# Expert rows and expert results as high and low fp32r parts

## The reference

```python
def moe_swiglu(h, w_router, w1, w3, w2):
    logits = (h @ w_router).astype(jnp.float32)
    top_v, top_i = lax.top_k(logits, TOP_K)
    gates = jax.nn.softmax(top_v, axis=-1)
    combine = jnp.sum(jax.nn.one_hot(top_i, N_EXPERTS, dtype=jnp.float32) * gates[..., None], axis=-2)
    out = jnp.zeros_like(h)
    for e in range(N_EXPERTS):
        out = out + combine[..., e:e + 1].astype(h.dtype) * swiglu(h, w1[e], w3[e], w2[e])
    return out
```

## Time and profile before

| | |
|---|---|
| time, median of 3 runs | 1761.59 us (1758.38 to 1762.69) |
| profiled execution | 1761.89 us |
| its span | 1760.0 us |
| TensorE matmuls | 1648.2 us busy, 94% |
| VectorE | 1336.6 us, 76% |
| ScalarE | 1059.4 us, 60% |
| GpSimd | 112.1 us, 6% |
| DMA | 427.99 MB, mean 243 GB/s |

### The profile page before, as it was taken

One profiled execution on the slowest core, in us unless ns is written; L12 is line 12 of the kernel. 1 busy time (PEld: TensorE's weight loads), 2 busy tenths in 40 slices (PEclk: granted clock), 3 DMA queues, 4 the chain that ended last, 5 costly groups with the idle time before them and its releaser, 6 DMA issues.

```text
span 1760.0 us, 27088 instructions
## 1 busy us (share of the span) xinstructions
PE 1648.2 (94%) x9618; PEld 1418.2 (81%) x9618; DVE 1336.6 (76%) x1250; ACT 1059.4 (60%) x1039; POOL 112.1 (6%) x151
## 2 busy tenths in 40 slices
PE   6888969999797897799999999999999999999997
PEld 5877859999797786688888888888888888888886
DVE  4888555444458865788888888888888888888885
ACT  4634454433353335477677677677777777676775
POOL 1142100000005210000000000000000000000000
PEclk8999989999899999799999999999999999999999
DMA  7520036452352103499999999999999999999993
GB/s 230 159 72 25 16 120 216 165 192 95 119 168 71 42 1 118 143 356 363 311 366 351 321 368 358 323 366 356 325 366 338 340 367 327 352 366 328 347 367 114
DMA packets 327137, 427.99 MB, mean 243 GB/s; under 512 B 6849, under 2 KB 294753, under 8 KB 326961
## 3 DMA queue, kind: packets, MB, share of 16 engines
q1 hardware_dynamic: 326304, 425.28, 71.8%
q0 software_dynamic: 640, 2.00, 0.4%
q10 hardware_dynamic: 144, 0.05, 0.0%
HBM read 426.25 MB, written 1.05 MB: 243 GB/s over the span
## 4 chain that ended last, share of the span: by engine, by line
PE 74%; DVE 11%; ACT 5%; issue 5%; DMA 4%; SPq 0%; DVEq 0%; ACTq 0%; POOL 0%; POOLq 0%
PE bank L375 29%; PE bank L400 15%; PE bank L1121 8%; PE bank L378 7%; PE bank L628 6%; PE bank L403 4%; DMA ring<-in_moe_w 3%; ACT wh L435 2%; DVE wl L439 2%; PE bank L660 1%; PE bank L388 1%; PE bank L1126 1%; DVE ml L615 1%; DVE hs L1877 1%; DVE rw L1779 1%
## 5 line engine op out<-in xcount | busy, mean ns | idle before, releaser
L439 DVE TENSOR_TENSOR wl<-ring,wh 128x2048 fp32r<-128x2048 f32 x369 | 844.6, 2293 | 211.4 <-ACT wh L435 198.8
L435 ACT ACTIVATE wh<-ring 128x2048 fp32r<-128x2048 f32 x369 | 705.9, 1915 | 130.2 <-PE bank L400 43.5
L375 PE MATMUL bank<-wh,xh 128*128 128x512 f32 x896 | 361.7, 404 | 0.9 <-DVE xl L868 0.9
L375 PE MATMUL bank<-wh,xl 128*128 128x512 f32 x896 | 351.1, 392 | 0.0
L375 PE MATMUL bank<-wl,xh 128*128 128x512 f32 x896 | 349.6, 390 | 0.0
L375 PEld LDWEIGHTS bank<-wh,xh 128*128 128x128 f32 x896 | 168.4, 188 | 37.5 <-issue 4.9
L375 PEld LDWEIGHTS bank<-wh,xl 128*128 128x128 f32 x896 | 168.3, 188 | 37.3
L375 PEld LDWEIGHTS bank<-wl,xh 128*128 128x128 f32 x896 | 169.0, 189 | 32.0
L400 PE MATMUL bank<-wh,gh 128*128 128x512 f32 x448 | 175.5, 392 | 3.5 <-DVE gl L525 3.4
L400 PE MATMUL bank<-wh,gl 128*128 128x512 f32 x448 | 174.6, 390 | 0.0
L400 PE MATMUL bank<-wl,gh 128*128 128x512 f32 x448 | 174.6, 390 | 0.0
(11 more groups left out here) (294 smaller groups left out, 2564.3 us busy)
## 6 DMA issues: line engine op xcount, KB each, us to landing
ring<-in_moe_w SPq DMA_DIRECT2D x336, 1024.0 KB, 8.3
ring<-in_ffn_w SPq DMA_DIRECT2D x33, 1024.0 KB, 6.1
ring<-in_w_in SPq DMA_DIRECT2D x24, 1024.0 KB, 5.3
ring<-in_w_out SPq DMA_DIRECT2D x8, 1024.0 KB, 5.1
ring<-in_w_in SPq DMA_DIRECT2D x2, 640.0 KB, 4.0
const<-in_const SPq DMA_DIRECT2D x1, 1200.0 KB, 14.4
proj<-in_x SPq DMA_DIRECT2D x4, 256.0 KB, 6.7
out<-wide SPq DMA_DIRECT2D x1, 1024.0 KB, 4.0
```

The lines of the kernel that those rows point to most:

```text
L375: ins = nc.tensor.matmul(up_bank(run, par, 0)[:], x[:, 0:C], w[b][:, k], **kw)
L435: nc.scalar.activation(o, src[0], ACT.Copy).then_inc(sem("w_high"), 1)
L439: nc.vector.tensor_tensor(split(wl[:, buf]), src[0], split(wh[:, buf]).bitcast(F32), ALU.subtract).then_inc(sem("w_split"), 1)
```

## The change

The rows of h are kept as two tiles, hh and hl, in fp32r, and gather multiplies both with `sel`, now fp32r. The gates leave the scatter matrix: `place`, the plain 0/1 sum, is transposed to `placed`, and the gate of each place comes as a column from two small matmuls of `selg` with ones, is copied to `gslot`, and is applied as a scale when the job's result leaves PSUM, again as two parts, yh (ScalarE) and yl (VectorE, new function `acc_low`). scatter multiplies both with `placed`. `zero_acc` is gone. The first down of a job, and of the dense layer, starts the sums itself, for which step 1 is taken out of the loop. The change's short description also names row-major weights; the diff changes no load of weights.

```diff
+        yh = sb("yh", [P, D], F32R)
+        yl = sb("yl", [P, D], F32R)
+        hh = sb("hh", [P, TT, D], F32R)
+        hl = sb("hl", [P, TT, D], F32R)
+        sel = sb("sel", [P, TT, C], F32R)
...
             n = run.pairs - 1
-            with pe.Fori(0, n // 2) as i:
-                step(2 * i + 1, 1)
+            step(1, 1, True)
+            with pe.Fori(0, (n - 1) // 2) as i:
                 step(2 * i + 2, 0)
-            if n % 2:
-                step(n, 1)
-
-        def zero_acc(banks_):
-            for b in banks_:
-                nc.tensor.matmul(bank[b][:], zeros[:, 0:P], zeros[:, P:P + 512], start=True, stop=True)
+                step(2 * i + 3, 1)
+            if (n - 1) % 2:
+                step(n, 0)
...
-            pe.wait_ge(sem("h_copied"), 4)
+            pe.wait_ge(sem("h_high"), 4)
+            pe.wait_ge(sem("h_low"), 4)
...
-                            mm(bank[5 + half][:, d * C:(d + 1) * C], hrows()[:, tt, k * P:(k + 1) * P], sel[:, tt],
-                               tt == 0, tt == 1, "gathered" if d == 3 and tt else None)
+                            mm(bank[5 + half][:, d * C:(d + 1) * C], hh[:, tt, k * P:(k + 1) * P], sel[:, tt], tt == 0, False)
+                            mm(bank[5 + half][:, d * C:(d + 1) * C], hl[:, tt, k * P:(k + 1) * P], sel[:, tt], False, tt == 1,
+                               "gathered" if d == 3 and tt else None)
...
-                    turn(bank[7][:, tt * P:(tt + 1) * P], selg[:, tt], sig="gates_turned" if tt else None)
+                    turn(bank[7][:, tt * P:(tt + 1) * P], place[:, tt])
+                for tt in range(TT):
+                    mm(bank[7][:, T:T + NE], selg[:, tt], cst("ones")[:, 0:NE], tt == 0, tt == 1, "gates_turned" if tt else None)
...
-                pe.wait_ge(sem("acc_copied"), 2 * j + 2)
+                pe.wait_ge(sem("y_low"), 2 * j + 2)
...
-                        mm(bank[SCATTER[b]][:, k * T:(k + 1) * T], yj[:, dt * P:(dt + 1) * P], pgt[:],
-                           sig="scattered" if k else None)
+                        mm(bank[SCATTER[b]][:, k * T:(k + 1) * T], yh[:, dt * P:(dt + 1) * P], placed[:], True, False)
+                        mm(bank[SCATTER[b]][:, k * T:(k + 1) * T], yl[:, dt * P:(dt + 1) * P], placed[:], False, True,
+                           "scattered" if k else None)
...
                 pe.wait_ge(sem("scatter_added"), 4 * (j - 1) + 2)
-                zero_acc((2, 3))
                 pe_steps(pe, nxt)
...
-                nc.scalar.copy(pgt[:], bank[7][:, 0:T]).then_inc(sem("gates_copied"), 1)
+                nc.scalar.copy(gslot[:], bank[7][:, T:T + 1]).then_inc(sem("gslot_ready"), 1)
+                nc.scalar.activation(placed[:], bank[7][:, 0:T], ACT.Copy).then_inc(sem("gates_copied"), 1)
...
-                    nc.scalar.copy(yj[:, half * 512:(half + 1) * 512], bank[2 + half][:]).then_inc(sem("acc_copied"), 1)
+                    nc.scalar.activation(yh[:, half * 512:(half + 1) * 512], bank[2 + half][:], ACT.Copy, scale=gslot[:, 0:1]
+                                         ).then_inc(sem("y_acc_high"), 1)
...
+            for b in range(4):
+                dve.wait_ge(sem("h_high"), b + 1)
+                hv = slice(b * T, (b + 1) * T)
+                nc.vector.tensor_tensor(hl[:, :, hv], bank[b][:].rearrange("p (a t) -> p a t", a=TT), hh[:, :, hv].bitcast(F32),
+                                        ALU.subtract).then_inc(sem("h_low"), 1)
...
+            def acc_low(j):
+                dve.wait_ge(sem("gslot_ready"), j + 1)
+                for half in range(2):
+                    dve.wait_ge(sem("y_acc_high"), 2 * j + half + 1)
+                    hv = slice(half * 512, (half + 1) * 512)
+                    nc.vector.scalar_tensor_tensor(yl[:, hv], bank[2 + half][:], gslot[:, 0:1], yh[:, hv].bitcast(F32),
+                                                   ALU.mult, ALU.subtract).then_inc(sem("y_low"), 1)
...
                 gathered(j)
                 up(0, 0, 0, 1)
+                acc_low(j - 1)
                 up(1, 0, 1, 0)
...
+                nc.gpsimd.tensor_tensor(place[:], hit[:, 0], hit[:, 1], ALU.add).then_inc(sem("gates_chain"), 1)
```

More of the change, by code:

```diff
@@ L178, in program @@
         hT = sb("hT", [P, KT, T])
-        zeros = sb("zeros", [1, 640], BF16)
         tiny = sb("tiny", [P, 1])
@@ L242, in program @@
         gate = sb("gate", [P, 2, T])
-        yj = sb("yj", [P, D])
-        sel = sb("sel", [P, TT, C])
+        yh = sb("yh", [P, D], F32R)
[3 more added lines that the diff above has]
+        sel = sb("sel", [P, TT, C], F32R)
+        place = sb("place", [P, TT, C])
+        gslot = sb("gslot", [P, 1])
         selg = sb("selg", [P, TT, C])
@@ L248, in program @@
         hit = sb("hit", [P, 2, TT, C])
-        pgt = sb("pgt", [P, T])
+        placed = sb("placed", [P, T], F32R)
         rt = sb("rt", [P, T])
@@ L389, in pe_turn_gated, with pe_down @@
                 ins.then_inc(sem("g_turned"), 1)
-        def pe_down(pe, run, m, last=False):
+        def pe_down(pe, run, m, last=False, first=False):
             stage, buf = run.down(m, last)
@@ L400, in pe_down @@
                             ins = nc.tensor.matmul(bank[2 + o][:], g[:, a, 0:C], w[b][:, a, o * 512:(o + 1) * 512],
-                                                   start=False, stop=False, skip_group_check=True)
+                                                   start=first and a == 0 and g is gh and b == 0, stop=False, skip_group_check=True)
                         else:
@@ L404, in pe_down @@
                                                    w[b][:, a, o * P:(o + 1) * P], g[:, a],
-                                                   start=False, stop=False, skip_group_check=True)
+                                                   start=first and o % 2 == a == b == 0 and g is gh, stop=False, skip_group_check=True)
                 if last and not run.moe and o % 2 and o < KT - 1:
@@ L410, in pe_steps, with step @@
         def pe_steps(pe, run):
-            def step(m, par):
+            def step(m, par, first=False):
                 pe_up(pe, run, m, par, 0)
@@ L415, in step @@
                 pe_up(pe, run, m, par, 1)
-                pe_down(pe, run, m - 1)
+                pe_down(pe, run, m - 1, first=first)
             n = run.pairs - 1
-            with pe.Fori(0, n // 2) as i:
-                step(2 * i + 1, 1)
+            step(1, 1, True)
+            with pe.Fori(0, (n - 1) // 2) as i:
                 step(2 * i + 2, 0)
-            if n % 2:
-                step(n, 1)
-        def zero_acc(banks_):
-            for b in banks_:
-                nc.tensor.matmul(bank[b][:], zeros[:, 0:P], zeros[:, P:P + 512], start=True, stop=True)
+                step(2 * i + 3, 1)
+            if (n - 1) % 2:
+                step(n, 0)
         def split_high(act, stage, buf, src, split):
@@ L552, in pe_ffn_dense @@
         def pe_ffn_dense(pe):
-            zero_acc((2, 3, 4, 5))
             for part in range(2):
@@ L687, in last_job @@
             return eng.value_load(jt[0:1, MAXJOBS + 1:MAXJOBS + 2], min_val=0, max_val=MAXJOBS - 2)
-        def hrows():
-            return wide[:].rearrange("p (a b) t -> p a (b t)", a=TT)
         def pe_moe(pe, mm, turn):
@@ L771, in act_moe @@
                 act.wait_ge(sem("h_turned"), b + 1)
-                copy(hrows()[:, :, b * T:(b + 1) * T], bank[b][:].rearrange("p (a t) -> p a t", a=TT), "h_copied")
+                nc.scalar.activation(hh[:, :, b * T:(b + 1) * T], bank[b][:].rearrange("p (a t) -> p a t", a=TT), ACT.Copy
+                                     ).then_inc(sem("h_high"), 1)
             act.wait_ge(sem("gate_logit"), 1)
@@ L784, in gates @@
                 act.wait_ge(sem("gates_turned"), j + 1)
-                nc.scalar.copy(pgt[:], bank[7][:, 0:T]).then_inc(sem("gates_copied"), 1)
+                nc.scalar.copy(gslot[:], bank[7][:, T:T + 1]).then_inc(sem("gslot_ready"), 1)
+                nc.scalar.activation(placed[:], bank[7][:, 0:T], ACT.Copy).then_inc(sem("gates_copied"), 1)
             def acc(j):
                 act.wait_ge(sem("stage_used"), job(j).down(0, True)[0] + 1)
+                act.wait_ge(sem("gslot_ready"), j + 1)
                 for half in range(2):
-                    nc.scalar.copy(yj[:, half * 512:(half + 1) * 512], bank[2 + half][:]).then_inc(sem("acc_copied"), 1)
+                    nc.scalar.activation(yh[:, half * 512:(half + 1) * 512], bank[2 + half][:], ACT.Copy, scale=gslot[:, 0:1]
+                                         ).then_inc(sem("y_acc_high"), 1)
             last = PAIRS_E - 1
@@ L923, in dve_moe @@
             dve_gated_low(dve, run, last)
+            acc_low(j)
             scattered(j)
@@ L937, in job_matrices @@
                                             ).then_inc(sem("gates_chain"), 1)
-                pool.wait_ge(sem("gates_chain"), 2 * j + 2)
+                pool.wait_ge(sem("gates_chain"), 3 * j + 3)
```

(1 more changed line is left out.)

## The result

The changed kernel takes 1770.78 us (median of 4 runs, 1766.73 to 1772.80), the kernel before 1760.15 beside it (4 runs, 1758.38 to 1762.69). The ratio is 1.0055 [1.0042, 1.0069], so +9.7 us; the two medians are 10.6 us apart. Measured again later on another chip, the changed kernel came out at 1.0044 [1.0027, 1.0061], +7.7 us. The prediction was 1789.3 in a range of 1759 to 1794. The sign was right, the size was not.

The account below looks back on a forecast made before the run. TensorE was taken as the bound, DMA some 6 us per job behind. Terms: 25.6 later downs, -2.3 release, +4.7 before job 0, -0.3 at the end: +27.7, so 1789.3 us; range 1759 to 1794, forecast's own 1784 to 1794.

Parts of the forecast that it names:

- I take 0.223: Gather: each 128-column fp32r matmul costs 0.223 us, as in fp32, so gather takes 7.14 us; held little better than even.
- +3.57 us: Gather at each of the 7 changes of job: TensorE time added by twice as many matmuls at 0.223 us.
- +3.7 at gather(0): Gather before job 0: about +3.7 us, from 0.223 us per matmul at full clock.
- rival A: Gather: 128-column fp32r matmuls cost 0.119 us, gather 3.81 us; sum +1.0, 1763 us; chance 0.36.
- That gather runs half on the slow clock: Gather before job 0: its 32 records take 5.93 us, half at the slow clock.
- Scatter gives nothing: Change of job: scatter's saving of 1.5 us becomes TensorE idle, about 2 us, before the wait for VectorE's second addition.
- The subtractions before job 0: VectorE, before gather(0): four subtractions of 128x512 delay the copy of the positions by 1.0 us.
- The scaled copies: ScalarE's two evacuations of results with a scale pointer: +0.09 us each, +0.2 on the chain per change of job.
- The low parts: VectorE, change of job: two scalar_tensor_tensor of 128x512 from PSUM take 1.4 us, falling into a 1.16 us gap plus 0.2.
- rival C: Change of job: short gather, but VectorE's two low parts find no gap, costing 1.5 us each time; 1773 us; chance 0.06.
- The release chain: Change of job, freeing banks 2 and 3: zeroing gone -0.53, ScalarE +0.2, so -0.33 us per change, -2.3 over 7.
- Rival B: Change of job: release of banks 2 and 3 does not hold TensorE, so scatter's saving counts; 1753 us; chance 0.08.

Follow-up runs that it names:

- The filler: Changed kernel plus 16 matmuls of 256 columns behind each scatter, written to bank 7, which nobody reads then: 1766.94 us, ratio 1.0033.
- the two kernels with filler: Changed kernel plus 16 extra matmuls behind scatter, with gather back in fp32 without subtractions (1761.72 us) or streaming 256 columns in 24 of 32 matmuls (1762.62 us).

## Why the prediction was wrong

**The failed step** is the gather: "I take 0.223". Measured: 0.112. The seven times +3.57 us never came (+0.03 each), and of the +3.7 at gather(0) +1.0 came. Together these terms were 28.7, more than the whole sum of +27.7. The argument "the only row of this very shape on four-byte data" put the shape above the format. The 32 fp32 records, each at 0.112, were already at the distance of the bare weight loads, 0.111: a row that shows a limit says nothing of the price per column beyond it. The Trainium skill's "TensorE: Matmul & The Clock Gate", section LDWEIGHTS, gives P/1.2 ns for a load of P columns, 107 ns for 128; the trace is near it, with 0.112 us over 32 pairs of load and matmul. I had cited it as the lower bound and then not let it decide.

That the sign came out right is luck. The time was forecast from a long gather, and what made the kernel slower is for the most part the clock, whose price the sum did not have. Only the 1.0 us of the subtractions was in it. The range holds the measured time only because it was drawn down to rival A; the forecast's own part of it began at 1784.

**Rival A had the right gather and missed the clock.** It gives 1763 and the median is 1770.8. "That gather runs half on the slow clock" took for granted that the clock would rise during the gather again (before, 4.5 of its 5.65 us were at the low level). With 128-column fp32r matmuls it did not: +1.0 us for the gather and +2.4 for job 0, shown by the gather alone in the old kernel (+5.1 with the subtractions) and taken away by 256 columns. That is 3.1 more than the 0.3 of rival A.

**The idle behind scatter was foreseen and priced at nothing.** "TensorE now idles about 2 us instead of 0.3. Scatter gives nothing" is right on both counts (2.08 us; from scatter to the next step −0.18). But the idle had a price of its own: in three of the profiles with it (one of them the changed kernel's second) the clock fell to 1.2 GHz right behind it, five times in all. The filler, which removes nothing but the idle, gives back 2.3, 3.3 and 5.5 us in three pairs of kernels, the last of them well clear of noise, the first not by itself. Not every such gap does it: the changed kernel's two profiles have seven each and show one fall behind them.

The Trainium skill's "TensorE: Matmul & The Clock Gate", section "Why this matters for your kernels", asks for no idle gaps between bursts of matmuls, with waits for DMA as its case, and the gaps that it warns of are longer than these. Here the clock also fell behind gaps of 2.1 us that a semaphore of VectorE makes, so the measurement decides.

**Steps that held.** The subtractions before job 0: +1.0 forecast, +0.98 measured. The scaled copies: yh 1.27 us for two against 1.07, +0.2 as forecast. The low parts: 1.41 for two, forecast 1.4, inside the gap; rival C is out. The release chain: −0.33 forecast, −0.18 seen. A quiet change in all −0.1 to −0.35, where rival A's terms (0.69 − 0.36 hidden − 0.33) make 0. Rival B is out as a forecast, since the second addition ends 3.9 us after scatter begins (1630.47 against 1626.58), but the wait that it names is where the time lies: with the wait moved, 8 us or so came back.

**How the 9.7 us divide.** By experiments: 4.4 to 5.1 for the gather's part (the gather alone), 2.3 to 5.5 for the clock behind the idle. What is left is about 2 us by the ratios, as in the two kernels with filler. The parts do not add up exactly: with the gather back in fp32 the ratio only went from 1.0055 or 1.0044 to 1.0036, less than the gather's part, and the two profiles of the changed kernel differ in where the clock falls. Part of the rest is the run's last stretch. After the last job TensorE waits 2.2 us for the low parts, and no filler stands there. In five of the ten profiles with this wait the clock falls again, 0.7 to 1.5 us after the wait ends. From the last transposes of gated values to the end these five take 25.5 to 25.6 us; the other profiles take 24.3 to 24.7. That was not tested alone. Also open: the profiles show one execution each, and how often the clock falls in the others can't be read, only that the changed kernel's mean clock is 0.968 to 0.971 against 0.972 to 0.976 before; and why in the first profile it fell at 1110.8, after an idle of 0.9 us, before scatter.

## What to carry to other kernels

When fp32 matmuls of few columns become pairs of fp32r matmuls, compare both with the distance of the bare weight loads first. Here both stood at that limit, and the change was worth nothing. Time saved on TensorE ahead of a fixed wait turns into idle, and the idle may be worse than the work it replaced, so move the wait to the first instruction that needs it in the same edit. And read the granted clock from window to window, not only its mean over the run: the changed kernel with its wait moved had a mean of 0.969 to 0.972, hardly above the changed kernel's, and took the time of the kernel before.

## What was not expected of the hardware

- An fp32r matmul of 128 columns with its load costs 0.112 us, at 256 columns 0.117 to 0.119: twice the columns for about 5% more. With the clock at half, the first is 0.213, as in gather(0) after:

```profile
725.25 0.42 PE L1142 MATMUL bank<-sel,hl 128*128 128x128 f32 x1
725.47 0.42 PE L1142 MATMUL bank<-sel,hh 128*128 128x128 f32 x1
```

- The high level comes at 726.2 to 729.2 us in all eight profiles with an fp32 or a 256-column gather, and at 737.1 to 739.4 in all five with the 128-column fp32r gather. At the low level TensorE was busy for 12.3 of 17.1 us in the changed kernel and 13.3 of 17.0 with the gather alone, against 4.4 of 6.8 before.
- Once the clock fell in the loop, it stayed at 1.2 GHz for 3.4 us of nearly full work and came back. The step behind scatter took 10.1 to 10.2 us with such a fall and 8.55 without, so one fall costs 1.6 us. The whole periods were 1.5 to 2.6 us longer, the longest of them with other waits in it.
